# Input projections computed wave by wave inside the expert stream, with the sums of the lots beside them on VectorE

## The reference, cut to what matters

```python
proj = rms_norm(x, norm_mix) @ w_in        # 1024 x 5128: FoX q|k|v|forget, SB q|k|v, two gates of 1024
fq, fk = rms_norm(fq), rms_norm(fk)        # per head of 64; 8 heads of each kind
c  = cumsum(log_sigmoid(ff + b_forget))    # over the rows, cached ones in front
o_fox = softmax(q.k/8 + c[t] - c[s]) @ v   # s <= t
o_sb  = stick_breaking(q.k/8) @ v          # s < t, reverse cumulative sum in log space
h  = x + (sigmoid(ga) * (o_fox @ w_o_fox) + sigmoid(gb) * (o_sb @ w_o_sb)) @ w_out
q  = rms_norm(h) @ w_peer_q                # 8 heads, two halves of 128
# top 16 of each half's 128 scores, top 16 of their 256 sums: 128 experts a row
out = h + sum over the 128 experts: softmax(score) * gelu(expert_u . n) * expert_v
```

## Time and profile before

| what | value |
|---|---|
| median of 3 runs (lowest, highest) | 4476.47 us (4464.86, 4478.14) |
| time of the profiled execution | 4467.62 us |
| its span from first to last instruction | 4465.8 us |
| PE, DVE, ACT, POOL busy | 3327.3, 2748.6, 1213.2, 1441.3 us |
| mean granted TensorE clock | 0.845 of full |
| bytes moved, mean rate | 1331.91 MB, 298 GB/s |

### The profile page before, as it was taken

How to read it: one execution, slowest core, us unless ns; L and a number is a source line. 1 busy time by engine, 2 the same in 40 slices (tenths; PEclk the granted TensorE clock), 3 DMA queues, 4 the chain that set the end, 5 groups by cost and what they waited for, 6 DMA issues and landing times.

```text
span 4465.8 us, 32784 instructions
## 1 busy us (share of the span) xinstructions
PE 3327.3 (75%) x10062; PEld 1690.7 (38%) x10062; DVE 2748.6 (62%) x5406; ACT 1213.2 (27%) x2631; POOL 1441.3 (32%) x1213
## 2 busy tenths in 40 slices
PE   6799997749895588789558888864777678745655
PEld 4334443434453244436224444531443234312222
DVE  2300000167549888747998885699766666997665
ACT  1111101215411365511126561111554431110110
POOL 0111001013222344423434442334333234444553
PEclk9999998667897788899779998987787789877787
DMA  3122111449986799999899999988887799989997
GB/s 125 55 76 94 58 73 38 148 172 364 354 306 239 278 416 416 386 376 392 324 347 407 407 371 390 395 340 326 322 339 302 301 375 368 400 308 378 420 420 324
DMA packets 251084, 1331.91 MB, mean 298 GB/s; under 512 B 29880, under 2 KB 73144, under 8 KB 104448
## 3 DMA queue, kind: packets, MB, share of 16 engines
q0 software_dynamic: 163232, 1142.47, 64.3%
q1 hardware_dynamic: 87680, 187.35, 11.7%
HBM read 1294.07 MB, written 35.10 MB: 298 GB/s over the span
## 4 chain that ended last, share of the span: by engine, by line
DVE 28%; PE 23%; DMA 14%; ACT 6%; issue 6%; SPq 3%; POOL 2%; ACTq 0%; DVEq 0%
DVE uv L1251 11%; DMA uv<-expert_uv,rows_u 9%; PE pv L871 9%; PE pb L980 4%; SPq L699 3%; DVE held L1277 3%; PE pb L953 3%; PE pb L928 2%; PE pb L853 2%; POOL uv L775 2%; PE pb L824 2%; DMA arena<-w_stream 1%; DMA arena<-out_sv_p 1%; DMA uv<-expert_uv,rows_pk 1%; DVE arena L1320 1%
## 5 line engine op out<-in xcount | busy, mean ns | idle before, releaser
L871 PE MATMUL pv<-uv,diag 128*128 128x512 f32 x2640 | 1504.9, 728 | 691.8 <-ACT diag L1095 617.6
L775 POOL DMA_INDIRECT uv<-expert_uv,rows_u x1024 | 1307.2, 1277 | 2075.9 <-PE pv L871 1367.0
L1251 DVE CUSTOM_DVE_ANT_0 uv<-uv,nr 128x1024 f32<-128x1024 f32 x1056 | 1240.8, 1220 | 203.2 <-DMA uv<-expert_uv,rows_u 168.3
L871 PEld LDWEIGHTS pv<-uv,diag 128*128 128x128 f32 x2640 | 600.1, 237 | 1486.6 <-issue 1411.6
L249 PE MATMUL ps<-win,xg 128*128 128x512 f32 (+1 forms) x1440 | 631.1, 597 | 0.0
L1102 ACT ACTIVATE gel<-dots 128x4 f32<-128x4 f32 x264 | 54.2, 205 | 1816.7 <-DVE dots L1251 1812.1
L1277 DVE SCALAR_TENSOR_TENSOR held<-uv,wgt,held 128x1024 f32<-128x1024 f32 x395 | 507.5, 1285 | 14.0 <-DVE wgt L1262 0.3
L824 PE MATMUL pb<-arena 64*128 64x512 f32 (+6 forms) x544 | 245.0, 560 | 203.7 <-DMA arena<-out_sv_p 124.5
L249 PEld LDWEIGHTS ps<-win,xg 128*128 128x128 f32 (+1 forms) x1440 | 261.1, 184 | 343.1 <-issue 342.9
L373 DVE TENSOR_SCALAR ffz<-ffz 128x72 f32<-128x72 f32 x1 | 0.2, 199 | 502.6 <-ACT ffa L315 502.6
L853 PEld LDWEIGHTS pb<-arena 128*128 128x128 f32 (+3 forms) x1728 | 211.4, 182 | 95.1 <-issue 63.5
(11 more groups left out here) (162 smaller groups left out, 2593.5 us busy)
## 6 DMA issues: line engine op xcount, KB each, us to landing
arena<-w_stream SPq DMA_DIRECT2D x80, 1024.0 KB, 8.8
win<-w_main SPq DMA_DIRECT2D x10, 2048.0 KB, 8.7
uv<-expert_uv,rows_u POOLq DMA_INDIRECT x1024
scratch_gates<-stage POOLq DMA_DIRECT2D x32, 256.0 KB, 2.3
arena<-scratch_gates SPq DMA_DIRECT2D x8, 1024.0 KB, 18.2
xg<-x_t SPq DMA_DIRECT2D x8, 536.0 KB, 7.7
arena<-scratch_c_p SPq DMA_DIRECT2D x8, 520.0 KB
xr<-x SPq DMA_DIRECT2D x8, 512.0 KB, 4.3
```

Source lines behind the costliest of these rows:

```text
L775: pool.indirect_dma_start(out=uv[k % NU][:].rearrange("p a n -> p (a n)"), out_offset=None, in_=io["expert_uv"][:, :], in_offset=bass.Indi ...
L871: mm = nc.tensor.matmul(pv[:, c * BANK:(c + 1) * BANK], diag[n % ND][:], uv[k % NU][:, 1, c * BANK:(c + 1) * BANK], start=n == first, stop ...
L1251: nc.vector.tensor_tensor_reduce(out=u, in0=u, in1=row[:], scale=1.0, scalar=0.0, op0=ALU.mult, op1=ALU.add, accum_out=dots[b % 2][:, k % ...
```

## The change

`project` as a stage of its own is gone. Each wave now begins, on every engine, with a `project(g)` of the tiles that it needs: `NEW` is (0, 8), (1, 2), (3, 4), (5, 6), (7,). The weights `w_main` are read again for each wave, as twenty halves of 1 MB (four k-steps by 512 columns) through the same ring of three that feeds the merge part. x comes in by wave (`load_rows`), into regions that the merge part has finished with. The banks of PSUM are `pb` 0 to 3 for two columns of up to two tiles, 4 for turned blocks and 5 for the forget gate. All stores that GpSimd made are now issued by SyncE, in its one list with the weight loads. The running sums are carried from wave to wave. The first pair of heads of a wave is loaded at column 7 of its projection, into a region of its own at the end of the arena; SyncE loads the rest after all that the projection stores has landed.

The ten columns of a projection are steps that take expert lots of the wave in front, each with a weight of 2.6 (1.3 for the single tile 7) against 1 for a step of attend or merge. Worked out from the new `Plan`, the lots are:

| beside wave | project | attend | merge |
|---|---|---|---|
| 1 | 9 | 12 | 11 |
| 2 and 3, each | 19 | 24 | 21 |
| 4 | 11 | 28 | 25 |

No lot lies beside column 0 of wave 1, one beside column 0 of waves 2 and 3, two beside each other column there. All four slots of a lot beside a projection are summed by VectorE: 232 slots in 58 lots, of which VectorE would have had 87 by the old rule. The 40 lots at the end are as before.

```diff
-def project(nc, io, dram, keep, consts):
-
-    cq = keep["cq"]
...
+QK = (0, 1, 3, 4)
+COLS = 10
+SCRATCH = ("q_fox", "k_fox", None, "q_sb", "k_sb")
+NEW = [tuple(t for sub in subs for t in sub) for subs in WAVES[:-1]] + [(TILES - 2,)]
+NEW[0] = (0, TILES - 1)
+STEP_LOTS = 2.6
...
-        self.lots = {}
+        self.lots, self.step_of = {}, {}
         for g in range(1, len(WAVES)):
-            steps = [("attend", g, s) for s in range(self.end[g] - self.first[g])]
-            steps += [("merge", g, s) for s in range(len(merge_steps(self.tiles[g])))]
+            steps = [(("project", g, c), STEP_LOTS * len(NEW[g]) / 2) for c in range(COLS)]
+            steps += [(("attend", g, s), 1) for s in range(self.end[g] - self.first[g])]
+            steps += [(("merge", g, s), 1) for s in range(len(merge_steps(self.tiles[g])))]
             first, count = self.tiles[g - 1][0] * LOTS, len(self.tiles[g - 1]) * LOTS
-            for i, step in enumerate(steps):
-                self.lots[step] = range(first + i * count // len(steps), first + (i + 1) * count // len(steps))
+            total, done = sum(w for _, w in steps), 0
+            for i, (step, w) in enumerate(steps):
+                a = first + int(done * count / total + 1e-6)
+                done += w
+                self.lots[step] = range(a, first + int(done * count / total + 1e-6))
+                for b in self.lots[step]:
+                    self.step_of[b] = step[0]
         self.rest = range(self.tiles[-1][0] * LOTS, ALL_SLOTS // LOT)
 
     def on_dve(self, k):
         j = k % NK
+        if self.step_of.get(k // LOT) == "project":
+            return True
         return j % LOT == 0 or (j % LOT == 1 and j // LOT % 2 == 1)
 
...
+        at[0] = ARENA - KINDS * (KS + 10 * PW + 2 * P)
+        kt0 = [carve(KS) for _ in range(KINDS)]
+        vt0 = [carve(10, PW) for _ in range(KINDS)]
+        qt0 = [carve(2 * P) for _ in range(KINDS)]
+        at[0] = 0
+        kt = [[kt0[k], carve(KS)] for k in range(KINDS)]
+        vt = [[vt0[k], carve(10, PW)] for k in range(KINDS)]
+        qt = [[qt0[k], carve(2 * P)] for k in range(KINDS)]
...
+        xt, xr = ot, xh
+        at[0] = gates_at
+        stage = [carve(BANK) for _ in range(4)]
+        sq = carve(BANK)
...
+                def load_half(g, c):
+
+                    n = chunk_no(g, c)
                     if n >= NW:
-                        wait_chunk_used(sp, *divmod(n - NW, CHUNKS))
-                    sp.dma_start(wring[n % NW], io["w_stream"][c]).then_inc(chunk_in[n % NW], 16)
-
-                for i, name in enumerate(("sub_keys_1_t", "sub_keys_2_t")):
...
+                def load_rows(g):
+
+                    if g:
...
+                    for c in range(NW):
+                        load_half(g, c)
+                    if not g:
+                        for i, name in enumerate(("sub_keys_1_t", "sub_keys_2_t")):
+                            sp.dma_start(skt[:, i, :], io[name]).then_inc(sk_in, 16)
+                    for c in range(COLS):
+                        for n in (2 * c + NW, 2 * c + 1 + NW):
+                            if n < 2 * COLS:
+                                load_half(g, n)
+                        store_stage(g, c)
+                        if c - 1 in QK:
+                            store_turned(g, c - 1)
+                        if c == 6:
+                            store_forget(g)
+                        if c == 7 and g:
+                            for i in range(2):
+                                sp.wait_ge(t_stored[i], proj.all_t[g][i])
+                            for ti in range(len(NEW[g])):
+                                sp.wait_ge(s_stored[proj.slot(4, ti)], proj.s_stored[g, 4, ti])
+                                sp.wait_ge(s_stored[proj.slot(5, ti)], proj.s_stored[g, 5, ti])
+                            load_pair(plan.first_pair[g])
+                    sp.wait_ge(proj_ready, proj.all_staged[g])
+                    sp.wait_ge(col_turned_out, proj.all_turned[g])
+                    sp.wait_ge(cq_out, tiles_to(g + 1))
+                    for i in range(4):
+                        sp.wait_ge(s_stored[i], proj.all_s[g][i])
+                    sp.wait_ge(v_stored, 16 * (tiles_to(g + 1) + 1))
+                    sp.wait_ge(c_stored, 16 * (g + 2))
...
                 for g, tiles in enumerate(plan.tiles):
-                    if g:
-                        sp.wait_ge(named, tiles[0])
+                    project(g)
                     for i, pair in enumerate(plan.pairs):
                         if pair[0] == g:
-                            load_pair(i)
+                            if g == 0 or i != plan.first_pair[g]:
+                                load_pair(i)
                             load_ck(2 * i)
...
+                    def column_half(c, half):
+                        n = chunk_no(g, 2 * c + half)
+                        pe.wait_ge(chunk_in[n % NW], 16 * (n // NW + 1))
+                        w = wring[n % NW].rearrange("p (k n) -> p k n", k=4)
+                        for ti, t in enumerate(tiles):
+                            r = rows_of(t)
+                            if c >= 2 and half == 0:
+                                pe.wait_ge(staged, proj.staged[g, c - 2, ti])
+                            for f in range(4):
+                                mm = nc.tensor.matmul(pb[0:r, proj.slot(c, ti), :], xt[:, half * 4 + f, ti * P:ti * P + r], w[:, f, :],
+                                                      start=half == 0 and f == 0, stop=half == 1 and f == 3)
+                            if half:
+                                mm.then_inc(proj_ready, 1)
+                        if half == 0:
+                            mm.then_inc(chunk_used, 1)
...
+                def store_stage(g, c):
+                    for ti, t in enumerate(NEW[g]):
+                        r, sem = rows_of(t), s_stored[proj.slot(c, ti)]
+                        row = stage[proj.slot(c, ti)]
+                        if c == 1:
+                            sp.wait_ge(normed, proj.normed[g, c, ti])
+                            store_rows(sp, (io["fk_p"], io["fk_s"]), row, t, sem)
...
+                        pe.wait_ge(s_used, banks_before(g))
+                        pe.wait_ge(q_out, wave_heads(g))
+                    else:
+                        pe.wait_ge(small_in, 96)
+                    pe.wait_ge(xg_ready, KD * (g + 1))
+                    forget()
+                    for c in range(COLS):
+                        for half in range(2):
+                            column_half(c, half)
+                            if c - 1 in QK and half < len(tiles):
+                                turn_column(c - 1, half)
+                        if c == 4:
+                            turn_logs()
+                        elif c == 6:
+                            turn_sums()
+                        beside(("project", g, c))
+
...
+                        ahead(("project", g, c))
+                        if c - 1 in QK:
+                            turn_out_column(c - 1, 0)
+                        for ti in range(len(tiles)):
+                            take_column(c, ti)
+                        if c - 1 in QK and len(tiles) > 1:
+                            turn_out_column(c - 1, 1)
+                        if c < 2:
+                            roots(c)
+                        elif c == 2:
+                            logs()
+                        elif c == 4:
+                            take_logs()
+                        behind(("project", g, c))
...
+                    for c in range(COLS):
+                        if c < 2:
+                            head_norms(c)
+                        if c == 1:
+                            forget()
+                        elif c == 3:
+                            logs()
+                        elif c == 5:
+                            running_sums()
+                        elif c == 7:
+                            take_sums()
+                        lots(("project", g, c))
```

598 lines of the change are left out of this document (294 added, 304 removed).

## The result

The changed kernel takes 4409.59 us (median of four runs, 4397.52 to 4426.14), the kernel before beside it 4477.31 (4464.86 to 4482.75). The ratio is 0.9855 with a 95% interval of 0.9813 to 0.9897: faster by 1.5%, where 3.2% was forecast. The profiled execution took 4417.6 us, its span is 4415.8.

The account below looks back on a forecast made before the run. It took expert gathers on DMA to set the pace after a front where DMA idles. 4465.8 - 580 (front) + 910 (projection steps) - 465 (lots leaving attend and merge) = 4331 us span, forecast 4335; range 4190 to 4480, own range 4240 to 4430.

Parts of the forecast that it names:

- Bound of the kernel now: Whole kernel: DMA idles while TensorE projects in the front; from 985 us on the expert gathers mostly set the pace.
- Part 3: Attend and merge of waves 1 to 4: 58 lots leave, -465 us, 8.0 a lot; ends 331 and 609.
- rival B: Attend and merge: freed lots leave steps whose own chains are as long, 331 instead of 465, 4465 us, no change; 8%.
- Part 1: Front: only tiles 0 and 8 projected ahead of wave 0, first scores at 195 us instead of 775, -580 us.
- Part 2: Projection steps of waves 1 to 4: 180, 280, 280 and 170 us, +910 us; ends 820 and 1080.
- The hole: Start of a wave's projection: VectorE's lots wait behind column 0's head norms, 43 us, 30 net in waves 2 and 3.
- ScalarE's loop: Projection steps: columns and lots taking turns because ScalarE's list couples them; denied ("I see no such loop"), D's far end.
- Part 4: Beside projections: 145 slots' sums go from TensorE to VectorE, 186 us already in part 2, hidden by the slots' DMA time.
- Part 5: SyncE's list: stores stand between weight loads, costed at nothing because TensorE is 1.5 columns ahead, about 20 us.
- rival D: Projection columns of waves 1 to 4: weight halves come late, 8 us a column, +320, 4650 us; 12%.
- A: Rival: DMA queue is all there is, holes vanish, each leaving lot worth nearly 10.5 us, total 4131, say 4160; 15%.
- C: Rival: TensorE at 1.2 GHz through the projection steps, waves 1 to 3 take 306 us each, total 4510, slower; 7%.

Follow-up runs that it names:

- half-bytes run: Gathers fetch 4 KB rows of u alone, v left out: 4223.92 us on the kernel before, 4039.66 us on the changed kernel.
- the old split: Changed kernel with sums beside projections shared as elsewhere, three of eight slots by VectorE, the rest by TensorE: 4396.38 us.
- the half dots: Changed kernel with each dot over the first 512 of its 1024 columns: 4277.17 us.

## Why the prediction was right, and where not

**Bound of the kernel now: the step that failed.** "The expert gathers set the pace" was read from DMA shares of 0.91 to 0.97, and made a lot worth 9 us in attend and 8 in merge. The half-bytes run of the kernel before shows otherwise: the same parts take 95 to 100% of their time with the share at 0.62 to 0.66. DMA's work and the engines' lists were both about as long as the stage; a lot taken off gives back what it takes on the longer of the two, and soon that is the lists. The prediction named this ("nearly level") and still took 9 and 8 us, in the upper half of what lay between its two bounds. For the 38 lots of waves 2 and 3 that made 324 us; 242 came, of which the lists alone are worth 217. The Trainium skill (Perfetto Trace Analysis, Identifying the Most-Contended Engine) says that the engine to work on is the one with the highest occupancy, and for DMA the utilization of its memory. By that rule too DMA would have been taken in attend, which ran at 392 GB/s, as the last lots do (385); the half-bytes runs do not bear it out there, save for 18 of 384 us in wave 2, while they do for the last lots.

**Part 3, sized at -465, was -382.** The mechanism, rival B's, took more than half of the way from 8.0 to 5.7: 6.6 a lot. Attend of wave 4 was right (450, forecast 466), for a reason of its own, the pairs that land late. Attend of waves 1 to 3 took 197, 306 and 340 instead of 188 (181 from the border at 985), 292 and 312. With the old split, and the same lots by the plan, attend takes 293 in wave 2, as forecast, and 325 in wave 3; the lot that runs on from the step in the change explains a part of that, though no run isolates it. In waves 1 and 3 one can see that even TensorE's list didn't shrink by 5.7 a lot: it was busy for 177.22 us in wave 1 and 295.36 in wave 3, where 193 - 29 = 164 (from 978 us on) and 331.52 - 57 = 275 were to be left. Its granted clock is 0.69 and 0.82 there, before it was 0.76 and 0.89, and 164 x 0.76 / 0.69 = 181 and 275 x 0.89 / 0.82 = 298 more than make up the difference; in wave 1 the same 224 matmuls of 128x64 took 322 ns each instead of 286. With fewer matmuls among its pauses TensorE was granted less of its two levels of 1.2 and 2.4 GHz. In waves 2 and 4 the clock held (0.85 and 0.84, 0.79 and 0.78), and the sum fits (255.30 against 256). That the lower clock made the stages longer is argued, not shown. Merge was 278, 345, 345 and 361; without the old holes the forecast is 1288 for the four, and 1330 came. There VectorE's list, choice of experts and dots together, is the longer one, as the half dots show.

**Part 1, -580, was -596.** First scores at 179 us instead of 195, TensorE busy for 154.78 of them at 0.99. The first matmul was at 14.4 us, where 20 to 25 were allowed for the loads, and TensorE then idled for 10 us, where 10 and 14 were allowed for norms and hand-over.

**Part 2, +910, was +940.** Its reasons held: DMA is the bound (780 instead of 1002 with half of the bytes), VectorE is under it (half dots change nothing), TensorE has room. In wave 2 DMA's own work was 0.88 x 298 = 262 us, forecast 247, and the rest is the time at both ends of the step when the queue runs dry. The steps took 206, 297, 298 and 200 us where 180, 280, 280 and 170 were said. The hole was named and sized at 43 us; filling it took 30, 26, 26 and 11 us off the four steps (80 off the whole), against the 30 net that the prediction put into waves 2 and 3. Its half clock came only for the forget matmuls (0.50 from 1042 to 1062 us); the first column ran at 0.92. What was denied is ScalarE's loop: gelus behind a column that is late. It shows as 345.0 us of waiting, and at 1302 to 1342, at a column's late weights; none of the runs isolates what it costs, and the one that reordered it was 27 us slower.

**Part 4, nothing, and about nothing it was** (13 us between the medians, in favour of the old split). **Part 5 and rival D:** a half lands after 13.5 us instead of 8.8, 5.8 with no lots beside the steps, and TensorE waits for it. But this wait is mostly slack: it fell by 163 us when TensorE had sums to do, and the time by at most 24. D's argument multiplied the landing time by 40 columns; loads overlap in the ring, and what counts there is DMA's total. What part 5 left out is that the first pair of heads stands on SyncE's list ahead of the last half, and that issuing it took SyncE 43 and 53 us in waves 2 and 3: "I cost it at nothing" had a reason for the stores, and none for this. TensorE's 82 us of waiting there may be lost or slack; no run tells. The Trainium skill (DMA: Bandwidth & Descriptors, Issuing engines are not separate DMA queues) says that transfers of different issuers interleave on the same engines; 5.8 against 13.5 us agrees.

**Rivals A and C.** A needed parts bound by DMA alone. C needed a clock under 0.6 in the columns: it was 0.86, 0.77, 0.78 and 0.73. The range (4190 to 4480) and the direction held, and 4410 lies even in the forecast's own range up to 4430; but the gain is less than half of the forecast. The lots' 465 - 382 = 83 us account for it; that the front (16 us better) and the steps (30 worse) nearly cancel is luck.

## What to carry to other kernels

A DMA share near 1 says that transfers fill the time, not that they set it: if an engine's list is as long, taking transfers away gives nothing. Halve the bytes with the same instructions and look at each stage before pricing a lot. When work is moved between stages, price it in both, and for the last piece moved rather than on average; and fill the hole at the start of a stage (here the next stage's first columns in the last stage's chain), which gave 80 us, where laying lots beside the projections had given some 20. Look, too, at what stands ahead of a load on the list of the engine that issues it: issuing can take long where the DMA engines are full.

## What the runs showed of the hardware

- A gather to the lower 64 partitions took as much DMA time as one to 128: 205 against 420 GB/s at a share of 1.0, so that an 8 KB packet on one of 16 engines took 16 x 8.19 / 205 = 0.64 us instead of 0.31. The Trainium skill (SBUF — State Buffer, Door 1) says that bandwidth depends on how many of 16 ports the partitions reach, and that partitions from 64 on use the other port of each cluster; by that rule the lower half reaches 8 ports and gets half of the rate, and the two rates here agree. The same number of bytes in 4 KB packets to 128 partitions took the queue 41.6% of 4040 us, where the changed kernel has 63.7% of 4416, 60% of the time for half of the bytes.
- Packets of 8 KB instead of 2 KB for 100 MB of weights brought the hardware queue's share from 19.4% to 18.9% and the landing from 13.5 to 11.0 us.
- TensorE's mean granted clock fell from 0.76 to 0.69 and from 0.89 to 0.82 in two attend stages that lost five and ten lots, and from 0.81 to 0.74 over the whole when half of its sum matmuls were left out, whose mean then rose from 725 to 897 ns. In two other stages that lost lots it held. Less work was thus not always as much less time.
- Issuing the eight loads of a pair of heads took SyncE 43 us (wave 2) and 53 us (wave 3) at a DMA share of 1.02, 8.5 us at a share of 0.89 and 5 us at 1.07 (wave 4). So it can take long where the engines are full, and need not; what decides is open.
